# A decoder layer with routed experts: last tile of tokens normed in plain order, last projection columns in a bank of their own, first weight homes freed by halves

## The reference

```python
def merge_and_ffn(...):
    m = g0 * (conv_out @ w_br_conv) + g1 * (attn_out @ w_br_attn) + g2 * (mem_out @ w_br_mem)
    h = layernorm(ALPHA * x + m @ w_o, ln1_g, ln1_b)
    return layernorm(ALPHA * h + hier_moe(h, ...), ln2_g, ln2_b)

def hier_moe(x, ...):            # 4 groups of 8 experts: best group, best 2 experts in it
    gsel = argmax(x @ w_group + b_group)
    pe = softmax(logits of the 8 experts of gsel);  top_p, top_i = top_k(pe, 2)
    gate = gw * top_p / sum(top_p)
    for e in range(32):          # w_up[e]: 1024 x 512, w_down[e]: 256 x 1024
        hu = x @ w_up[e]
        y += gate[:, e] * ((silu(hu[:, :256]) * hu[:, 256:]) @ w_down[e])
```

## Time and profile before

| | |
|---|---|
| median of 3 runs | 582.14 us (581.97 to 582.24) |
| the profiled execution | 585.24 us |
| its span | 583.4 us |
| TensorE busy | 528.5 us (91%) |
| VectorE busy | 280.6 us (48%) |
| moved | 163.44 MB, mean 280 GB/s |

### The profile page before, as it was taken

The page is one execution under the profiler, slowest core; times in us unless marked ns, Lnnn a source line. Parts: engine busy times, 40 slices in busy tenths (PEclk is TensorE's granted clock), DMA queues, the critical chain, the costliest instruction groups (busy, mean ns, idle before and its releaser), DMA issues.

```text
span 583.4 us, 8621 instructions
## 1 busy us (share of the span) xinstructions
PE 528.5 (91%) x3492; PEld 321.4 (55%) x3492; DVE 280.6 (48%) x786; ACT 103.5 (18%) x245; POOL 48.9 (8%) x58
## 2 busy tenths in 40 slices
PE   7999999999999999999999998899999795985781
PEld 4556566556477787888776556455555251521220
DVE  1273857689789894975552597411012000101017
ACT  1001111011324325332100231111111010101021
POOL 0000000000020435431000000000000000000003
PEclk9999999999999999999999999999999898998896
DMA  8990432746365466675879947799999999999962
GB/s 286 397 343 3 144 104 79 280 162 207 113 243 157 132 230 208 233 245 181 338 284 408 332 156 312 259 424 420 422 420 420 421 422 421 422 421 422 414 244 76
DMA packets 48430, 163.44 MB, mean 280 GB/s; under 512 B 5986, under 2 KB 22844, under 8 KB 36356
## 3 DMA queue, kind: packets, MB, share of 16 engines
q1 hardware_dynamic: 39824, 139.81, 62.4%
q0 software_dynamic: 3472, 14.31, 7.0%
q10 hardware_dynamic: 5092, 8.74, 4.2%
HBM read 160.05 MB, written 2.77 MB: 279 GB/s over the span
## 4 chain that ended last, share of the span: by engine, by line
PE 54%; DVE 19%; DMA 18%; ACTq 5%; issue 2%; ACT 1%; SPq 1%; DVEq 0%
DMA ring<-in_w_up 16%; PE bank L802 13%; PE bank L625 10%; PE bank L1180 6%; PE bank L572 3%; PE bank L673 2%; ACTq L1567 2%; PE bank L1287 2%; ACTq L1566 2%; PE bank L1155 2%; PE bank L1137 2%; PE bank L1215 2%; DVE proj L1769 2%; DVE ring L1769 2%; DVE gates L1899 2%
## 5 line engine op out<-in xcount | busy, mean ns | idle before, releaser
L625 PE MATMUL bank<-ring,work 128*128 128x512 f32 (+2 forms) x224 | 91.8, 545 | 1.5 <-DMA ring<-in_w_in 1.5
L802 PE MATMUL bank<-work,ring 128*128 128x264 f32 x384 | 90.1, 390 | 0.0
L802 PEld LDWEIGHTS bank<-work,ring 128*128 128x128 f32 x384 | 71.3, 190 | 14.5 <-issue 2.5
L1180 PE MATMUL bank<-ring,work 128*32 128x512 f32 x320 | 55.8, 670 | 18.1 <-DMA ring<-in_w_up 14.9
L625 PEld LDWEIGHTS bank<-ring,work 128*128 128x128 f32 x224 | 39.6, 190 | 30.0 <-issue 26.8
L2429 DVE SCALAR_TENSOR_TENSOR work<-work,bank 128x256 f32<-128x256 f32 x8 | 3.4, 421 | 88.1 <-ACT work L1627 88.1
L2441 DVE COPY gates<-bank 128x512 f32<-128x512 f32 x8 | 5.5, 691 | 74.2 <-PE bank L1287 65.4
L1180 PEld LDWEIGHTS bank<-ring,work 128*32 128x32 f32 x320 | 15.5, 121 | 45.7 <-issue 45.5
L945 PE MATMUL bank<-work,ring 128*128 128x264 f32 x128 | 31.4, 391 | 0.7 <-ACT gates L1472 0.6
L945 PEld LDWEIGHTS bank<-work,ring 128*128 128x128 f32 x128 | 23.4, 190 | 8.7 <-issue 3.4
L1180 PE MATMUL bank<-proj,work 128*32 128x512 f32 x112 | 25.3, 593 | 1.2 <-DMA ring<-in_w_up 1.2
(11 more groups left out here) (350 smaller groups left out, 828.6 us busy)
## 6 DMA issues: line engine op xcount, KB each, us to landing
ring<-in_w_up SPq DMA_DIRECT2D x20, 2048.0 KB, 23.8
ring<-in_w_in SPq DMA_DIRECT2D x21, 1024.0 KB, 5.5
ring<-in_w_down SPq DMA_DIRECT2D x8, 2048.0 KB, 23.1
proj<-in_w_up SPq DMA_DIRECT2D x6, 2048.0 KB, 24.4
extra<-in_w_up SPq DMA_DIRECT2D x3, 2048.0 KB, 24.3
ring<-in_w_o SPq DMA_DIRECT2D x4, 1024.0 KB, 10.1
extra<-in_w_down SPq DMA_DIRECT2D x2, 2048.0 KB, 19.9
proj<-in_w_down SPq DMA_DIRECT2D x2, 2048.0 KB, 32.8
```

The costliest lines, as they stand in the source:

```text
L625: last = mm(bank[2 * (i % 2) + t][:, 0:w], lhs[:, k, 128 * t:128 * t + 128], rhs[:, k % 4, :], start=(k == 0), stop=(k == KT - 1))
L802: last = mm(b[:, 0:TOK], w[:, k, 128 * (n % 2):128 * (n % 2) + 128], xT[:, k, 0:TOK], start=(k == 0), stop=(k == KT - 1))
L1180: last = mm(bank[5][32 * j:32 * j + 32, :], xTe[q // 2 % 2][:, k, s0:s0 + CAP], up_of(n + j // 2, j % 2, r), start=(k == 0), stop=(k == KT ...
```

## The change

1. `ln_scale_turned` is gone. Tile 1's last norm step writes plain order straight into `h3[:, 1]`, once, and all gathers read tile 1 through `h_rows`, every eighth word. `residual_tile(1)` reads `h3[:, 1]`.
2. Tile 1's projection is in three parts: columns 0 to 511 in bank 2, 512 to 767 in bank 3, 768 to 1023 in bank 7, with a sum, a count of `wo_ps`, statistics and turned blocks for each; the last two turned blocks go through bank 2.
3. Homes 0 and 1 are loaded for their second use by halves (`unit_rows`, 1024 KB in 4 KB rows). The first half waits for `half_used`, counted after two of the four row steps of `up_half(0, 0)`, the second for `used_w` as before.
4. `down_0[1]` is issued behind these four halves; half of home 8 waits for `hp_ready` 3 in place of `h_ready` 3; `route_ready` is counted before the gates of the first pair; the count of tokens goes to bank 3 and is read after `first_slots(1)`, and TensorE waits for it before `residual_tile(1)` rather than before `up_half(0, 0)`.

```diff
+        def h_rows(t, k):
+            return h3[:, 1, k:D:KT] if t == 1 else h3[:, t, 128 * k:128 * k + 128]
...
+            def unit_rows(w, u, e0, half):
+                e = e0 + 2 * (u % 2)
+                at = (2048 * (u // 2) if u < UPS else 0) + 1024 * half
+                s = (w_up if u < UPS else w_dn)[e:e + 2, :, :].rearrange("j (p r) n -> p j (r n)", p=128)
+                d = wslot[w].rearrange("p (j n) -> p j n", j=2)
+                sp.dma_start(d[:, :, 1024 * half:1024 * half + 1024], s[:, :, at:at + 1024]).then_inc(quad_in[w], 16)
...
                 if p == 7:
-                    sp.wait_ge(wo_ps, 4)
+                    sp.wait_ge(wo_ps, 5)
                 if p == 8:
...
-                    sp.wait_ge(h_ready, 3)
+                    sp.wait_ge(hp_ready, 3)
                 if p == NWS:
-                    sp.wait_ge(route_ready, 1)
-                    sp.dma_start(down_0[1], e0[:, 1]).then_inc(aside_in, 16)
+                    for i in range(2):
+                        sp.wait_ge(half_used, i + 1)
+                        unit_rows(i, units[p + i] % WPQ, 4 * (units[p + i] // WPQ), 0)
...
+                elif NWS <= p < NWS + 2:
+                    unit_rows(w, n % WPQ, 4 * (n // WPQ), 1)
+                    if p == NWS + 1:
+                        sp.wait_ge(route_ready, 1)
+                        sp.dma_start(down_0[1], e0[:, 1]).then_inc(aside_in, 16)
...
+            W_PARTS = ((2, 0, 512), (3, 512, 256), (7, 768, 256))
+
+            def wo_second(part, ks):
+                b, c0, w = W_PARTS[part]
                 for k in ks:
+                    last = mm(bank[b][:, 0:w], mT[k][:, 128:256], wo(k)[:, c0:c0 + w], start=(k == 0), stop=(k == 6))
                 return last
...
             pe.wait_ge(r_ready, 3)
-            r_turn(1, 0)
+            r_turn(1, 5, 0, 4)
             wo_second(1, (4, 5, 6)).then_inc(wo_ps, 1)
+            wo_second(2, (4, 5))
             pe.wait_ge(r_ready, 4)
-            r_turn(1, 1)
+            r_turn(1, 6, 4, 6)
+            wo_second(2, (6,)).then_inc(wo_ps, 1)
             pe.wait_ge(ht_sb, 4)
             logits(1, bank[5][:, 0:36], 0, 4)
             pe.wait_ge(ht_sb, 5)
-            logits(1, bank[5][:, 0:36], 4, KT).then_inc(lg_ps, 1)
+            logits(1, bank[5][:, 0:36], 4, 6)
+            pe.wait_ge(r_ready, 5)
+            r_turn(1, 2, 6, 8)
+            pe.wait_ge(ht_sb, 6)
+            logits(1, bank[5][:, 0:36], 6, KT).then_inc(lg_ps, 1)
...
-            pe.wait_ge(cnt_read, 1)
...
+                        if q == 0 and b == 0 and r == 1 and j % 2 == 1:
+                            last.then_inc(half_used, 1)
...
             dve.wait_ge(wo_ps, 4)
-            residual(1, 1, r_ready)
-            link(V.bn_stats(stats[:, 6:12], h3[:, 1, 512:1024]))
-            link(V.bn_aggr(stats[:, 46:48], stats[:, 0:12]))
+            residual(1, 3, 512, 256, r_ready)
+            link(V.bn_stats(stats[:, 12:18], h3[:, 1, 512:768]))
+            dve.wait_ge(wo_ps, 5)
+            residual(1, 7, 768, 256, r_ready)
+            link(V.bn_stats(stats[:, 18:24], h3[:, 1, 768:1024]))
+            link(V.bn_aggr(stats[:, 46:48], stats[:, 0:24]))
...
             route(LATE, 1)
-            ln_scale_turned(ytmp, 1, lnb, hp_ready)
+            ln_scale(ytmp, 1, lnb, h3[:, 1, :], hp_ready)
             dve.wait_ge(pos_ps, 2)
             places(LATE, bank[5][:, 64:96].unsqueeze(1))
             first_slots(0, LATE, 1)
-            link(V.tensor_reduce(rt[:, 143:144], bank[5][:, 96:128], AX.X, ALU.max), cnt_read)
-            ln_scale(ytmp, 1, lnb, h_ready)
             tt(eg, lgg, b3(m3, 4), ALU.subtract)
             link(V.tensor_reduce(m1, les, AX.X, ALU.max))
             tt(e8, les, b3(m1, 8), ALU.subtract, e_ready)
             first_slots(1, ALL3, 3)
+            dve.wait_ge(pos_ps, 3)
+            link(V.tensor_reduce(rt[:, 143:144], bank[3][:, 0:32], AX.X, ALU.max), cnt_read)
```

More of the change, by code:

```diff
@@ L337, in landed @@
         def landed(w, uses):
-            return 16 * (2 * uses if w == NWS - 1 else uses + 1 if w == NWS - 2 else uses)
+            return 16 * (2 * uses if w == NWS - 1 else uses + 1 if w == NWS - 2 or w < 2 and uses > 1 else uses)
         def run_uses(w):
@@ L1028, in residual_tile @@
             def residual_tile(t):
+                h = h3[:, 1, :] if t else ytmp
                 for dh in range(2):
-                    last = mm(bank[2 * t + dh][:, :], alpha_id, ytmp[:, 512 * dh:512 * dh + 512], start=True, stop=False)
+                    last = mm(bank[2 * t + dh][:, :], alpha_id, h[:, 512 * dh:512 * dh + 512], start=True, stop=False)
                 return last
@@ L1040, in _ @@
             pe.wait_ge(r_ready, 1)
-            r_turn(0, 0)
-            r_turn(0, 1)
+            r_turn(0, 5, 0, 4)
+            r_turn(0, 6, 4, 8)
             wo_second(0, (2, 3))
-            wo_second(1, (0, 1))
+            for part in (1, 2):
+                wo_second(part, (0, 1))
             pe.wait_ge(h_ready, 1)
@@ L1048, in _ @@
             pe.wait_ge(r_ready, 2)
+            pe.wait_ge(ht_sb, 1)
             for k in range(KT):
-                last = tr(bank[7][:, 8 * k:8 * k + 8], h3[0:NS, 2, 128 * k:128 * k + 128], NS)
+                last = tr(bank[5][:, 8 * k:8 * k + 8], h3[0:NS, 2, 128 * k:128 * k + 128], NS)
             last.then_inc(ht_ps, 1)
-            wo_second(1, (2,))
+            for part in (1, 2):
+                wo_second(part, (2,))
             pe.wait_ge(c_ready, 1)
@@ L1062, in _ @@
             residual_samples().then_inc(res_ps, 1)
-            wo_second(1, (7,))
+            for part in (1, 2):
+                wo_second(part, (7,))
             mask = rt[:, 0:96]
@@ L1093, in _ @@
             mm(bank[5][:, 64:96], ones[:, 0:128], mask[:, 0:32], start=False, stop=False)
-            mm(bank[5][:, 64:96], ones[:, 0:128], mask[:, 64:96], start=False, stop=True)
+            mm(bank[5][:, 64:96], ones[:, 0:128], mask[:, 64:96], start=False, stop=True).then_inc(pos_ps, 1)
             for t in range(3):
-                last = mm(bank[5][:, 96:128], ones[:, 0:128], mask[:, 32 * t:32 * t + 32], start=(t == 0), stop=(t == 2))
+                last = mm(bank[3][:, 0:32], ones[:, 0:128], mask[:, 32 * t:32 * t + 32], start=(t == 0), stop=(t == 2))
             last.then_inc(pos_ps, 1)
@@ L1580, in std, with h_turned @@
                 act.activation(stats[0:m, 40 + t:41 + t], stats[0:m, 36 + t:37 + t], ACT.Sqrt).then_inc(std_ready, 1)
[L1582 to L1586, removed]
+            def h_turned(i, t, b, k0, k1):
+                act.wait_ge(ht_ps, i)
+                act.activation(hT[:, k0:k1, 128 * t:128 * t + 128],
+                               bank[b][:, 0:128 * (k1 - k0)].rearrange("p (k n) -> p k n", k=k1 - k0), ACT.Copy)\
+                    .then_inc(ht_sb, 1)
             def h_copied(n, t, m):
@@ L2372, in _ @@
             dve.wait_ge(wo_ps, 3)
-            residual(1, 0, r_ready)
-            link(V.bn_stats(stats[:, 0:6], h3[:, 1, 0:512]))
+            residual(1, 2, 0, 512, r_ready)
+            for i in range(2):
+                link(V.bn_stats(stats[:, 6 * i:6 * i + 6], h3[:, 1, 256 * i:256 * i + 256]))
             dve.wait_ge(pos_ps, 1)
```

60 lines of the change are left out of this document (28 added, 32 removed).

## The result

The changed kernel takes 584.59 us (median of 11 runs, 582.79 to 585.88), the kernel before 582.20 beside it (11 runs). The ratio is 1.0031, with a 95% interval of 1.0017 to 1.0045: 1.8 us slower (the medians alone are 2.4 apart; differences between kernels are taken from the ratios here). The forecast was 581.2, its range 578.6 to 582.8; both were wrong.

The account below looks back on a forecast made before the run. The queue of expert weights was taken to bound the kernel through its restart time. A restart 1.1 us earlier, less 0.2 for smaller rows, gave -0.9 off the median 582.14: 581.2 us, range 578.6 to 582.8.

Parts of the forecast that it names:

- What bounds the kernel: Expert phase: the weight queue sets the end by how early it runs full, 421 GB/s, and by never running dry.
- 1 us earlier is 1 us off the end: Restart of home loads after the gap: each us earlier shortens the kernel equally if nothing starves the queue after.
- The restart: First half of home 0 after the gap: issued at 370.33 instead of 371.46 with slow strided loads, 1.1 us earlier.
- the upper bound of 250: Tile 1's strided gather loads: at most 250 ns each, from VectorE's wide-stride turned scale; 230 was taken.
- the break-even of 288: Tile 1's sixteen strided gather loads: above 288 ns each, 4.61 us in all, the restart would come later than before.
- What is late next: down(0) waiting for the moved down_0[1]: TensorE 2.8 us late, 3.7 with strided gathers, 4.6 of margin used, queue not starved.
- The margin of 5.6 us: Later home issues: 5.6 us to spare before the queue empties at 400.2, and 5.6 again at 430.1.
- rival 3: Tile 1's gathers: strided loads well over 250 ns, at 340 ns queue 2.6 us past its margin, 584.7 us; chance 0.15.
- rival 1: Tile 1's gathers: strided loads free or hidden, -2.8 us, 579.3 us; chance 0.30.
- rival 2: Free strided loads, and halves queued while leftovers still move, sparing the slow start after a stop; 578.3 us; chance 0.07.
- rival 4: Home 0 and 1 loads: halving does nothing, for instance held up in the queue, and loads are slow; 582.1 us; chance 0.05.

Follow-up runs that it names:

- e5: Kernel before with only down_0[1] moved behind homes 0 and 1, no halves; ratio 1.0043 to the kernel before.
- e8: Changed kernel with seven dropped products of 512 columns before TensorE's wait for down_0[1]; ratio 1.0062 to the kernel before.
- e2: Kernel before with the halves alone, no norm part, route_ready counted before the gates, down_0[1] behind the four halves; ratio 1.0002 to the kernel before.
- e4: Changed kernel with tile 1's turned write and contiguous loads back, plain scale after first_slots(1), down_0[1] still behind the halves; ratio 0.9997 to the kernel before.
- e10: e1 with tile 1's gathers reading adjacent words of the plain order, so its feature order differs from the reference's; ratio 0.9957 to the kernel before.
- e1: Changed kernel with down_0[1] put back in front of the four half transfers; 580.16 us against 582.43 for the kernel before, ratio 0.9948.
- e9: Changed kernel with three dropped products of 512 columns before TensorE's wait for down_0[1]; ratio 0.9992 to the kernel before.
- e6: e1 with tile 1's turned write and contiguous loads back, as in e4, plain scale after first_slots(1); ratio 0.9977 to the kernel before.
- e11: e1 with one turned write of tile 1, contiguous gathers and a residual streamed with a stride of 128 words; ratio 0.9975 to the kernel before.
- e7: e1 without the third bank, the projection in two parts of 512 columns as before; ratio 0.9984 to the kernel before.
- e12: e7 without the halves; ratio 0.9988 to the kernel before.
- e3: Kernel before with the halves alone, no norm part, route_ready counted before the gates, down_0[1] in front of the halves; ratio 0.9994 to the kernel before.

## Why the prediction was wrong

**What bounds the kernel: right.** The rate is flat from the restart on unless the queue runs dry, and the lost flow goes with the ratio: the three slowest kernels (changed, e5, e8) lost 1.1 to 4.0 us of it, and the six with ratios under 0.999 lost none; e2 and e4 lost 1.0 to 1.1 us at a ratio of 1.000. The step from there to "1 us earlier is 1 us off the end" is not borne out: e10's restart is 3.1 us earlier than e1's and worth nothing that the ratios show.

**The restart: right, in part by luck.** Forecast mark + 23.45 for the first half (370.33 less 346.88), measured 23.6. The strided loads were 260 ns apart, above the upper bound of 250 that I took from VectorE's row and under the break-even of 288; `up_half` started just where I had put it, since two errors cancel: the gathers took 0.4 us longer than forecast and began 0.4 us earlier, most of it from the bank (0.6 us on VectorE for the 0.26 that I counted). The Trainium skill's rule (SBUF — State Buffer, the note on cachelines in "Door 1: The DMA port swizzle") that a wide stride pays was borne out, 335 ns a load against 192 for contiguous ones, both at a granted clock of 1.00 (e8 and the kernel before).

**What is late next: the step that failed.** I wrote that "the change uses 3.7 + 0.9 = 4.6 of it with slow loads" and "neither starves the queue". The margin of 5.6 us was right; what was charged to it was too small:

| term, us | forecast | measured |
|---|---|---|
| restart earlier | 0.9 | 1.0 |
| `down(0)` starts late | 2.8 | 3.8 |
| `down(0)` lasts longer | 0 | 1.7 |
| the two gathers behind it | 0.9 | 1.0 |
| sum | 4.6 | 7.5 |

7.5 - 5.6 = 1.9 us past the margin; the dip at 396 is 3 x (421 - 188) / 421 = 1.7, and the second, behind sixteen more strided loads, 0.6. The same sum tells where the other kernels stand: it gives 6.6 for e2, 6.5 for e4 and e5, 9.2 for e8 and 5.8 for e9, past the margin by 1.0, 0.9, 0.9, 3.6 and 0.2, and they lost 1.1, 1.0, 1.1, 4.0 and 0.5 us of flow; for e1 it gives 3.1, within the margin, and e1 lost none. The term that I had not seen is the third: I priced the wait by its length alone, and not the work behind it at the lower clock. e9 takes that term away and loses 0.5 us of flow for 2.4; e1 takes the wait away and loses none; e5 makes the wait alone (with its first large transfer 0.6 us later) and is slower. The second term was off by 1.0: from the first half's issue to the landing I had 10.2 + 1.25 + 2.45 = 13.9 us and it took 383.0 - 368.5 = 14.5; the first half went 0.13 later than forecast, and TensorE began 0.25 behind the landing.

**The rivals.** The time of rival 3, 584.7, is the median measured (the ratio makes it 583.9), and its end (the queue past its margin) is what happened. Its cause was not: the loads did not cross 288 ns, and the restart was earlier, not later. I had made the dry queue hang on the stride alone. Rivals 1, 2 and 4 did not come about. e10, which is rival 1's condition with `down_0[1]` in front, measured 2.5 us under the kernel before, but e1, with slow loads, is as fast: the 1.9 us that I gave to free loads (2.8 less 0.9) are not seen.

**The sum.** One us of restart won and 2.4 lost make +1.4; the ratio says +1.8 (1.0 to 2.6). The profile of one execution, mark to end, has +0.4. The bytes explain part of this: of the 190 us behind the mark, the kernel before lost 10.7 us of full flow, the changed one 11.6 and e1 8.9. The changed kernel had gained 1.5 us by mark + 32, more than the 1.0 of its first half home, and then lost 2.3; net that is 0.8 us slower. I do not explain the us between this and the ratio. For e1 the same sum, against the changed kernel, is 2.4 (no dry queue) + 1.25 (the leftover in the hole) - 0.8 (home 0 later in its profile) = 2.9, and 236.9 - 234.0 is 2.9; the ratios say 4.8.

**Open.** Three things: what holds the queue near 300 GB/s for some 5 us behind a restart (297 in e10, 279 before); why the earlier restarts of e6, e10 and e11 make none of them faster than e1; and the last 1 to 2 us between ratios and profiles.

## What to carry to other kernels

Where a small transfer is moved behind large ones, follow it to its reader, and charge the stand there with what follows it: in this kernel a wait of 3.3 us on TensorE cost 1.7 more in the products behind it. Hold all that is late against the margin at which the queue runs dry, as one sum; here the queue had 5.6 us in hand, and what went past that was lost flow. And try a change's parts in another order before you drop it: the same edits with one leftover in front of the halves are the fastest kernel here, 0.52% under the kernel before (0.26 to 0.77%).

## What the runs showed of the hardware

At a granted clock of 1.00 a weight load that takes every eighth f32 word lasts 335 ns for 192 with adjacent words. At 0.50 the stride costs a load next to nothing: strided loads last 334 to 340 ns there (changed kernel), those with adjacent words 333 (e4). A moving operand of 512 columns with a stride of 128 words makes the instruction 1040 to 1109 ns long (e11), and the four of the residual 3.71 us for 1.98.

The granted clock fell to 0.50 at each stand of 3.3 to 5.5 us at `down(0)` (changed kernel, e2, e4, e5; in e4 and e5 while TensorE still stood, in the other two within 0.5 us of its start), and at that place in none of the nine others and not in the kernel before. An earlier fall, beginning somewhere in 357 to 366 us, was there in nine profiles (changed, e1 to e4, e7, e9, e11, e12) and not in before, e5, e6, e8 and e10. e2 and e3 execute the same instructions as the kernel before up to that place, so it needs no edit; what makes it was not found. In six of the nine it lies over tile 1's gathers or the start of `up_half(0, 0)`, in e12 over the gathers before them, and it delays home 0 (by 0.8 us in e1, by some 2.4 in e12).
